# Storing the split weights of the first tile and loading them in the four later tiles

## The reference, cut to what matters

```
h = rmsnorm(x) * norm_g
z = h @ w_in                       # 1024 x 5120: q f i g | u b | ma mb
o = HGRN2(q, f, i)                 # gated linear recurrence, 4 heads, chunks of 32
y_a = (rmsnorm(o) * silu(g)) @ w_proj_a
y_b = (pool_mix(u) * silu(b)) @ w_proj_b
out = x + (sigmoid(ma) * y_a + sigmoid(mb) * y_b) @ w_out
y = rmsnorm(out);  also the new recurrent states and pooling buffers
```

## Time and profile before

| | |
|---|---|
| median of 3 runs | 1419.71 us (1419.51 to 1420.68) |
| the profiled execution | 1421.46 us |
| its span, first to last instruction | 1419.7 us |
| TensorE busy | 1391.7 us (98%) |
| VectorE, ScalarE, GpSimd busy | 900.8, 691.3, 241.3 us |
| DMA | 179.16 MB, mean 126 GB/s |
| mean granted TensorE clock | 0.997 |

### The profile page before, as it was taken

The page is one execution under the profiler, slowest core; times in us unless marked ns, Lnnn a source line. Parts: engine busy times, 40 slices in busy tenths (PEclk is TensorE's granted clock), DMA queues, the critical chain, the costliest instruction groups (busy, mean ns, idle before and its releaser), DMA issues.

```text
span 1419.7 us, 22385 instructions
## 1 busy us (share of the span) xinstructions
PE 1391.7 (98%) x8428; PEld 1373.8 (97%) x8428; DVE 900.8 (63%) x1457; ACT 691.3 (49%) x1021; POOL 241.3 (17%) x230
## 2 busy tenths in 40 slices
PE   6999999999999999999999999999999999999996
PEld 5999999999999999999999999999999999999996
DVE  6778644558885456688744457886445597774444
ACT  5656533455664344556633436665334464553332
POOL 1102122111130211111212110112220210130003
PEclk9999999999999999999999999999999999999998
DMA  4332453334236333343363334334533453334337
GB/s 154 113 102 91 157 168 116 108 127 153 75 105 215 119 107 117 108 151 93 101 214 111 114 106 127 131 105 134 178 121 104 127 163 130 114 121 167 114 106 85
DMA packets 53937, 179.16 MB, mean 126 GB/s; under 512 B 13888, under 2 KB 14144, under 8 KB 52160
## 3 DMA queue, kind: packets, MB, share of 16 engines
q1 hardware_dynamic: 53824, 177.64, 40.3%
HBM read 166.46 MB, written 11.16 MB: 125 GB/s over the span
## 4 chain that ended last, share of the span: by engine, by line
PE 92%; DVE 3%; ACT 2%; DMA 1%; issue 1%; SPq 0%; DVEq 0%; ACTq 0%
PE Z L420 28%; PE Z L422 28%; PE Z L421 28%; PE B L552 1%; PE B L512 1%; PE B L475 1%; PE B L542 1%; ACT whi L660 1%; DMA ss_out<-snew 1%; DVE wlo L851 1%; PE B L462 1%; DVE xres L1162 1%; DMA xin<-xT 0%; PE B L466 0%; PE B L532 0%
## 5 line engine op out<-in xcount | busy, mean ns | idle before, releaser
L851 DVE TENSOR_TENSOR wlo<-wraw,whi 128x1024 fp32r<-128x1024 f32 x280 | 368.0, 1315 | 392.8 <-ACT whi L660 392.7
L420 PE MATMUL Z<-hhi,whi 128*128 128x416 f32 x1584 | 562.4, 355 | 1.5 <-DVE wlo L851 0.9
L422 PE MATMUL Z<-hhi,wlo 128*128 128x416 f32 x1584 | 552.3, 349 | 0.0
L421 PE MATMUL Z<-hlo,whi 128*128 128x416 f32 x1584 | 552.2, 349 | 0.0
L660 ACT ACTIVATE whi<-wraw 128x1024 fp32r<-128x1024 f32 x280 | 295.6, 1056 | 456.7 <-PE Z L422 429.0
L420 PEld LDWEIGHTS Z<-hhi,whi 128*128 128x128 f32 x1584 | 297.5, 188 | 5.3 <-issue 4.1
L421 PEld LDWEIGHTS Z<-hlo,whi 128*128 128x128 f32 x1584 | 297.6, 188 | 2.0 <-issue 1.9
L422 PEld LDWEIGHTS Z<-hhi,wlo 128*128 128x128 f32 x1584 | 297.3, 188 | 0.3
L422 PE MATMUL Z<-mhi,wlo 128*128 128x416 f32 x320 | 112.3, 351 | 0.0
L421 PE MATMUL Z<-mlo,whi 128*128 128x416 f32 x320 | 111.9, 350 | 0.0
L420 PE MATMUL Z<-mhi,whi 128*128 128x416 f32 x320 | 111.5, 348 | 0.0
(11 more groups left out here) (212 smaller groups left out, 1645.0 us busy)
## 6 DMA issues: line engine op xcount, KB each, us to landing
wraw<-w_all SPq DMA_DIRECT2D x280, 512.0 KB, 3.5
xres<-xT SPq DMA_DIRECT2D x5, 1664.0 KB, 7.4
xin<-xT SPq DMA_DIRECT2D x4, 1664.0 KB, 7.8
yT<-xres SPq DMA_DIRECT2D x4, 1664.0 KB, 6.6
s<-s_in SPq DMA_DIRECT2D x4, 512.0 KB, 5.4
ss_out<-snew SPq DMA_DIRECT2D x4, 512.0 KB, 5.1
xin<-xT SPq DMA_DIRECT2D x4, 416.0 KB, 5.5
yT<-xres SPq DMA_DIRECT2D x3, 416.0 KB, 2.5
```

Of the source, the lines that this page charges most:

```text
L420: pe.matmul(out, wh, xh, start=first, stop=False)
L421: pe.matmul(out, wh, xl, start=False, stop=False)
L422: return pe.matmul(out, wl, xh, start=False, stop=final)
L851: dve.tensor_tensor(wlo[n % RING][:], wraw[n % RAW][:], whi[n % RING][:].bitcast(F32), ALU.subtract).then_inc(wlo_made, 1)
```

## The change

In tile 0 everything is split as before, and SyncE also stores each `whi` and `wlo` block (512 KB each) in a buffer in device memory, `parts_of`. In tiles 1 to 4 no raw block is loaded and nothing is split: SyncE loads the two stored parts straight into the rings, three units ahead, and TensorE waits for their landing. A ring buffer is refilled when the unit that used it is done, so SyncE's slot s now begins at Ts in tiles 1 to 4. Two groups of DMAs of the last tile are moved to other slots.

```diff
+        part_stored = [sem(f"part_stored{i}") for i in range(RING)]
+        part_landed = [sem(f"part_landed{i}") for i in range(RING)]
+        parts_of = nc.dram_tensor("weight_parts", (NU, 2, P, D), F32, kind="Internal").ap()
...
-        def landed(t, n):
-            return 16 * (t * (NU // RAW) + n // RAW + 1)
+        def landed(n):
+            return 16 * (n // RAW + 1)
+        def stored(n):
+            return 32 * (n // RING + 1)
+        def parts_ready(engine, t, n):
+            if first(t):
+                engine.wait_ge(wlo_made, n + 1)
+            else:
+                engine.wait_ge(part_landed[n % RING], t * (32 * (NU // RING)) + 32 * (n // RING + 1 - NU // RING))
...
             def tile(t, last):
                 for s in range(NU):
-                    n = s + RAW
-                    if n < NU or not last:
-                        sp.wait_ge(wlo_made, nth(t, NU, s))
-                        sp.dma_start(wraw[n % RAW][:], w_all[n % NU]).then_inc(w_landed[n % RAW], 16)
+                    if first(t):
+                        sp.wait_ge(wlo_made, s + 1)
+                        if s + RAW < NU:
+                            sp.dma_start(wraw[s % RAW][:], w_all[s + RAW]).then_inc(w_landed[s % RAW], 16)
+                        for part, src in enumerate((whi, wlo)):
+                            sp.dma_start(parts_of[s, part],
+                                         src[s % RING][:].bitcast(F32)).then_inc(part_stored[s % RING], 16)
+                    n = s + AHEAD
+                    if (n >= NU or not first(t)) and (n < NU or not last):
+                        sp.wait_ge(acc_done, t * NA + (LAST_ACC[s - 1] + 1 if s else 0))
+                        sp.wait_ge(part_stored[n % RING], stored(NU - 1))
+                        for part, out in enumerate((whi, wlo)):
+                            sp.dma_start(out[n % RING][:].bitcast(F32),
+                                         parts_of[n % NU, part]).then_inc(part_landed[n % RING], 16)
...
-                    if s == 14 and last:
+                    if s == 12 and last:
                         sp.wait_ge(y_stored, 16 * (TILES - 1))
                         sp.dma_start(s0[1][:], s_in[1]).then_inc(s0_landed[1], 16)
-                    if last and s in (15, 19, 23, 27):
-                        h = (s - 15) // 4
+                    if last and s in (10, 14, 18, 22):
+                        h = (s - 10) // 4
...
-                    pe.wait_ge(wlo_made, nth(t, NU, s))
+                    parts_ready(pe, t, s)
...
         def _(act):
-            def split(t, n):
-                act.wait_ge(w_landed[n % RAW], landed(t, n))
+            def split(n):
+                act.wait_ge(w_landed[n % RAW], landed(n))
+                if n >= RING:
+                    act.wait_ge(part_stored[n % RING], stored(n - RING))
                 act.activation(whi[n % RING][:], wraw[n % RAW][:], ACT.Copy).then_inc(whi_made, 1)
...
-                    if s + AHEAD < NU or not last:
+                    if first(t) and s + AHEAD < NU:
                         act.wait_ge(acc_done, t * NA + (LAST_ACC[s - 1] + 1 if s else 0))
-                        split(t, s + AHEAD)
+                        split(s + AHEAD)
...
         def _(dve):
-                    if s + AHEAD < NU or not last:
-                        split(t, s + AHEAD)
+                    if first(t) and s + AHEAD < NU:
+                        split(s + AHEAD)
```

More of the change, by code:

```diff
@@ L601, in tile @@
                         if i == 0:
-                            pe.wait_ge(wlo_made, nth(t, NU, s + 1))
+                            parts_ready(pe, t, s + 1)
                             for u in range(2):
@@ L829, in _ @@
                     act.activation(lb[:, 3:5], lb[:, 3:5], ACT.Exp).then_inc(lbe_made, 1)
-            split(0, 0)
+            split(0)
             x_norm(1)
@@ L834, in _ @@
                 if k == 2:
-                    split(0, 1)
+                    split(1)
                 h_hi(1, k, h0[k])
             for n in range(2, AHEAD):
-                split(0, n)
+                split(n)
             act.wait_ge(lb_made, LB_STEPS)
@@ L847, in _, with split @@
         def _(dve):
-            def split(t, n):
-                dve.wait_ge(whi_made, nth(t, NU, n))
+            def split(n):
+                dve.wait_ge(whi_made, n + 1)
                 dve.tensor_tensor(wlo[n % RING][:], wraw[n % RAW][:], whi[n % RING][:].bitcast(F32),
```

## The result

The changed kernel takes 1432.1 us (median of 4 runs, 1430.52 to 1434.46) against 1419.8 for the kernel before. The ratio on record is 1.0084, 95% interval 1.0072 to 1.0096 (the two medians alone give 1.0087). It is slower by 12 us where 2 us less was forecast, and above the range. All differences in this document are under 1%; they can be read because the executions of one kernel mostly lie within 0.3% of each other.

A forecast was written before the change was run, and what follows sets the result against it. TensorE's single stream of matmuls, with 3.1 us of holes, was taken as the bound. Holes removed -3.1, tile 0 stores 0, later loads 0, `s0[1]` wait +1.1: -2.0 us, so 1417.7 us, range 1415.8 to 1427.

The forecast's parts named there:

- the waits for `ktm` and `snew`: TensorE waits in the last tile, 1.0 and 0.6 us, put down to splits and forecast to go.
- Cost in tile 0: nothing: Tile 0's 112 added stores: at 400 GB/s the T28 to T54 stretch fits, so 0 us; upper end 14.
- the rival of a DMA-bound first tile: Tile 0: stores mixed with loads fall below the needed rate; 1424 us at 330 GB/s, 1432 at 312; chance 0.18.
- 346: Tile 0, T28 to T54: the GB/s below which the DMA-bound first tile would decide.
- 358 GB/s: The Trainium skill's bound on HBM to SBUF transfers; by it tile 0's dense stretch ends 7 us late, still hidden.
- The ring's 11 us: Tile 0: a split can lose 11 us before TensorE sees it, so a backlog of 8.5 us stays hidden.
- nine microseconds of slack from the banks alone: Tile 0: banks read by ScalarE's work behind a late split are wanted two units (9 us) later.
- -0.9 - 0.6: TensorE's waits at tile starts, 0.9 us for `wlo` and 0.6 us "issue", counted as the splits' and forecast to go.
- +1.1: Last tile, head 1: a new TensorE wait of 1.1 us for `s0[1]`, loaded after the output store; ends 0 and 5.
- the upper end of 5: Last tile: `s0[1]` wait of 5 us if store and load are each 2 us slower; 1421.6 us, within the 0.56 forecast.
- `xin` is late and hidden: Tiles 1 to 3: ScalarE waits ten microseconds longer in slot 28, hidden from TensorE with 2.7 us to spare.
- the estimate: Whole kernel after the change: VectorE near 606 and ScalarE near 455 us busy.

The follow-up runs named there:

- Experiment 11: Changed kernel, loop written out, output store earlier, no stores or loads of parts, no splits in tiles 1 to 4 (stale weights): 1416.24 us.
- Experiments 1: Kernel before, with only the stores of tile 0 added, and ScalarE's wait for them before it splits into a buffer again: 1427.77 us.
- 2: Changed kernel, storing only units 52 to 55, which tiles 1 to 4 load instead (wrong weights), without ScalarE's wait for the stores: 1426.48 us.
- 9: Changed kernel, loop written out, early output store, first eight units not stored but loaded raw and split again in every later tile: 1416.80 us.
- 12: Kernel of experiment 5, with the stores of tile 0 issued by ScalarE on its own DMA queue instead of SyncE's: 1424.55 us.
- experiments 3: Changed kernel, with the loop over tiles 1 to 3 written out on all engines: 1427.34 us.
- 4: Kernel before, with the loop over tiles 1 to 3 written out on all engines: 1418.63 us.
- experiment 8: Kernel before, with its loop, also storing the parts of units 0 to 3 in tiles 1 to 4, around the jump: 1424.17 us.
- 10: Changed kernel, with its loop; SyncE's loads of slots 54 and 55 moved to slot 0, so DMA is quiet around the jump: 1431.17 us.
- experiment 5: Changed kernel, loop written out; in the last tile the output store moved to slot 9 and the `s0[1]` load to slot 11: 1422.55 us.

## Why the prediction was wrong

**The bound was right, the gain small.** TensorE's stream of matmuls sets the time, its pace did not change under three times the traffic (270 matmuls in 50 us at 134 and at 389 GB/s, below), and the waits for `ktm` and `snew` went, worth 1.0 us between tile 3 and the last, and part of 1.2 us in the last tile. Experiment 11 confirms a ceiling of some 2 us. That leaves no room for any loss, and there were three.

**The step that failed: "Cost in tile 0: nothing".** Its rate was about right, 400 GB/s taken and 389 measured. This is a window of the dense stretch, before and after, with the columns of the earlier trace rows:

```profile
180.00:230.00 50.00, 50.00 (x270) 50.00 (x269) 23.79 (x23) 18.91 (x27) 12.48 (x10) 1.00 0.42 134
180.00:230.00 50.00, 50.00 (x270) 50.00 (x269) 20.66 (x22) 19.93 (x30) 10.47 (x8) 1.00 1.00 389
```

389 GB/s at full share, and TensorE never idle: neither 346 nor 358 GB/s was the limit. That the measured 1432.1 us is what the rival of a DMA-bound first tile gives at 312 GB/s is chance: the loss lies elsewhere.

What failed was the choice of place. I weighed the stores where most bytes per unit fall (T28 to T54), and asked only when the weights and the banks are wanted. The loss is made at the very start, where the splits have to fill the ring and follow faster than every 4.48 us. In the kernel before, ScalarE begins the splits of blocks 4 to 7 at 30.74, 33.53, 37.12 and 39.52 us, one in 2.9 us. With the stores a unit is 1.573 MB, and at 400 GB/s that takes 3.9 us (an estimate from rows 4); in the changed kernel they begin at 30.55, 34.34, 38.91 and 42.62, one in 4.0 us. DMA is full all the while: from 26 to 50 us its share is 1.00, where it was 0.40 before. SyncE's and ScalarE's timelines of the changed kernel, from 36 us:

```profile
36.68 0.33 SPq L368 DMA_DIRECT2D wraw<-w_all  x1
...
42.62 1.06 ACT L687 ACTIVATE whi<-wraw 128x1024 fp32r<-128x1024 f32 x1 [2.24 <-issue]
43.58 0.50 ACT L713 ACTIVATE h_ga<-Z 128x416 f32<-128x416 f32 x1
44.10 1.28 ACT L768 ACT_TABLE_LOAD   x1
45.40 0.73 ACT L718 ACTIVATE h_logf<-h_sf,lb 128x416 f32<-128x416 f32 x1
```

Raw block 7 is issued at 36.68 and takes 5.9 us, to 42.6. ScalarE has stood in slot 4 for it for 2.24 us (the view says "issue"; the landing is what ends then). The change also makes this split wait for the stores of block 3, but they aren't what held it: the last was issued at 28.80 and took 8.9 us, to 37.7. Behind that split, in program order, stand the sigmoid of g, the table load and the logarithm: the head of a chain through both engines that ends in `kj`, which TensorE wants in slot 7. In the kernel before that split began at 39.52, the chain ended at 51.35, and TensorE came for it at 51.77: no idle time, and 0.4 us of slack.

```profile
39.52 1.06 ACT L660 ACTIVATE whi<-wraw 128x1024 fp32r<-128x1024 f32 x1 [0.94 <-DMA wraw<-w_all]
...
50.80 0.55 DVE L941 TENSOR_TENSOR kj<-h_e,dec 128x384 f32<-128x384 f32 x1
...
51.77 0.49 PE L512 MATMUL B<-ident,kj 128*128 128x128 f32 x3
```

Now it ends at 54.4, 3.1 us later, and TensorE is there at 50.4:

```profile
54.48 0.70 PE L537 MATMUL B<-ident,kj 128*128 128x128 f32 x3 [4.08 <-DVE kj L968]
```

Of the 4.08 us of idle time, 2.7 are delay (54.48 against 51.77) and the rest is that TensorE came 1.4 us earlier: its matmuls left the low clock of the start sooner in this profile. Another 1.6 us are lost between there and slot 8, at a low clock: 7.72 us in place of 6.14.

The ring's 11 us protect the weights. They do nothing for the work that is queued behind the late split. I had named it ("ScalarE's other work stands behind the late split") and then gave it nine microseconds of slack from the banks alone. Experiments 1 and 2 show that the stores do it, 9 that it is those of the first eight units, and 12 that it is traffic and not queue order.

**The term "-0.9 - 0.6" was not the splits'.** It is the jump back of the loop (experiments 3, 4). With transfers around it TensorE stands for up to 2.2 us; with DMA quiet, for 0.4 (8, 10). In the changed kernel SyncE issues the parts of the next tile's unit 2 at 568.04 us, they keep DMA busy until 572.1, TensorE stops at 572.5, and the next pair is issued at that moment. This is 1.5 us of gain that did not come and 2.8 of new loss. The Trainium skill has the mechanism, in "Runtime: NRT & Kernel Launch", section "Instruction fetch mechanics": a taken branch out of the current window forces a DMA fetch of the target before execution goes on. The runs agree as far as they go: without the branch the holes are gone. I had not weighed it. That other traffic lengthens the hole is these runs' finding; that a hole is the wait for such a fetch is not shown: the only packet of an instruction queue in the changed kernel's first hole, 572.5 to 574.7 us, moved at about 572.9, long before the end.

**The term "+1.1" for `s0[1]` was too small.** It measured 4.3 us (experiment 5, against the same tile without it), within the upper end of 5 that the prediction kept. The mechanism was the one forecast, and the profile has it in the chain that ended last:

```profile
1184.55 11.30 DMA yT<-xres
1195.87 4.12 DMA s<-s_in
1200.03 2.15 PE B L587 x16
```

The store was issued 0.85 us after T11 (1183.70), behind the two loads of unit 14, and took 11.3 us; I had worked out 9.4 from T11. The load took 4.1, not 5.4. Together that makes the idle time 2.4 in place of 1.1. The rest is the clock: it was 0.70 and then 0.87 in the two stretches of 4 us behind the hole, which by an estimate from these two costs 4 x 0.30 + 4 x 0.13 = 1.7 us; with the 2.4 that is 4.1 of the 4.3. I counted idle time at its face value.

**Right:** `xin` is late and hidden. ScalarE waits 46.6 us for it in four tiles, 14.0 at the longest, and TensorE not at all. The busy times of VectorE and ScalarE came out 12 and 21 us above the estimate.

## What to carry to other kernels

Before trading engine work for traffic, look up how long the bound engine waits for that work: here 2 us, and a single stray wait eats that. Weigh a new stream of transfers where the schedule has no slack, at the start and at the head of each chain, and not where its mean rate is highest; follow everything that stands in program order behind the one wait it lengthens. And a wait that the profile puts down to a producer at a loop's start may be the jump's own.

## What the runs showed of the hardware

A jump back of a loop on all engines left TensorE idle for 0.4 us with DMA quiet for 6 us ahead of it, 0.6 to 0.9 in the kernel before, 1.5 to 2.0 with 1 MB of stores added around it (experiment 8), and 2.1 to 2.2 in the changed kernel, where DMA was full until 0.5 us ahead.

Idle time can cost more than itself. After the 4.1 us without a matmul in tile 0 of the changed kernel the granted clock was 0.59 in the window of the next four, and in the last tile 0.70 after 2.4 us of idle time with few matmuls around it, against 1.00 elsewhere: parts of these stretches ran at 1.2 in place of 2.4 GHz.

```profile
50.00:54.00 4.00, 0.40 (x3) 0.05 (x1) 3.93 (x9) 3.88 (x7) 1.28 (x2) 1.00 0.39 161
54.00:58.00 4.00, 3.52 (x51) 3.01 (x52) 2.47 (x4) 0.10 (x1) 0.00 (x0) 0.59 0.74 242
...
1200.00:1204.00 4.00, 3.97 (x19) 2.94 (x20) 3.83 (x14) 0.00 (x0) 0.00 (x0) 0.70 0.34 139
```

In the holes of the jumps of 2.2 and 2.1 us it stayed at 1.00, and from the second matmul behind them on they start 0.19 us apart, as elsewhere.

At the kernel's start the clock's column can't be trusted. Between 18 and 22 us it has 1.00 for the kernel before and 0.50 for experiment 8, with 11 matmuls in both. The starts of the matmuls tell more: they are 0.35 us apart until 22.8 us in the kernel before and until 20.4 in the changed one, and 0.19 from there on. How long the slow spacing lasts there differs from run to run: in ten of the profiles it ends between 18.5 and 23.6 us.

Left open: why slot 8 of tile 0 begins anywhere between 62.2 and 64.2 us in the five profiles that have all the stores on SyncE's queue. Up to 1.6 us of it is there when the split of block 7 begins (42.62 us in the changed kernel, 44.20 in experiment 5), and up to 1.1 is how long the low clock lasts behind the wait for `kj` (7.7 us from its end to slot 8 in one, 8.8 in another). It is not in when the first x blocks land: they land soonest in experiment 5, 6.0 us after issue, and its split is the latest. No run separated the causes.
